# Gate and linear projections of two feed-forward blocks: seven half-width products in place of eight, on weight sums made by VectorE

## What is computed

```python
def swiglu(h, w_gu, w_dn):                       # h (512, 1024), w_gu (1024, 5632), w_dn (2816, 1024)
    g, u = jnp.split(h @ w_gu, 2, axis=-1)
    return (jax.nn.silu(g) * u) @ w_dn

x = x + 0.5 * gt1 * rmsnorm_2(swiglu(h, w_gu1[l], w_dn1[l]), g_post[l, 0])
...
x = x + 0.5 * gt3 * rmsnorm_2(swiglu(h, w_gu2[l], w_dn2[l]), g_post[l, 2])
```

## Time and profile before

| what | value |
|---|---|
| median of 3 runs | 2291.43 us (2290.36 to 2295.13) |
| the profiled execution, its own time | 2295.32 us |
| span of that execution in the profile | 2293.3 us |
| TensorE clock granted, mean | 0.987 of full |
| PE busy, share of the span | 2258.4 us, 98% |
| POOL busy | 1056.0 us, 46% |
| DVE busy | 1015.3 us, 44% |
| ACT busy | 902.7 us, 39% |

### The profile page before, as it was taken

How to read it: one execution, slowest core, us unless ns; L and a number is a source line. 1 busy time by engine, 2 the same in 40 slices (tenths; PEclk the granted TensorE clock), 3 DMA queues, 4 the chain that set the end, 5 groups by cost and what they waited for, 6 DMA issues and landing times.

```text
span 2293.3 us, 32856 instructions
## 1 busy us (share of the span) xinstructions
PE 2258.4 (98%) x10438; PEld 1858.3 (81%) x10438; DVE 1015.3 (44%) x1670; ACT 902.7 (39%) x1632; POOL 1056.0 (46%) x812
## 2 busy tenths in 40 slices
PE   8999999999999999999999999999999999999997
PEld 7888888888888888888888778888677787888886
DVE  6899785527623415110115235555565555100112
ACT  4334663333222333332333354444665453332332
POOL 3455555454444454444445443333322454444444
PEclk8999999999999999999999999999999999999999
DMA  4333444337747532333332323334312432333331
GB/s 150 97 97 96 145 120 158 96 107 288 269 134 230 174 97 78 93 100 97 96 96 83 84 80 111 110 110 142 97 51 60 149 95 74 96 96 97 96 97 60
DMA packets 129483, 263.95 MB, mean 115 GB/s; under 512 B 14256, under 2 KB 14384, under 8 KB 128624
## 3 DMA queue, kind: packets, MB, share of 16 engines
q1 hardware_dynamic: 119520, 236.51, 34.4%
q10 hardware_dynamic: 9872, 26.25, 3.0%
HBM read 250.02 MB, written 12.58 MB: 115 GB/s over the span
## 4 chain that ended last, share of the span: by engine, by line
PE 89%; DVE 5%; issue 3%; ACT 2%; POOL 1%; DMA 0%; ACTq 0%; DVEq 0%; POOLq 0%
PE bank L1028 25%; PE bank L1030 25%; PE bank L1029 25%; PE bank L1293 2%; PE bank L1294 2%; PE bank L1295 2%; PE bank L1383 1%; PE bank L1346 1%; PE bank L1427 1%; POOL wlo L415 1%; PE bank L1449 1%; DVE bank L1712 1%; PE bank L1368 1%; PE bank L1168 0%; PE bank L1131 0%
## 5 line engine op out<-in xcount | busy, mean ns | idle before, releaser
L415 POOL TENSOR_TENSOR wlo<-raw,whi 128x512 fp32r<-128x512 f32 x750 | 985.9, 1323 | 1135.2 <-ACT whi L517 1134.1
L1028 PE MATMUL bank<-a_hi,whi 128*128 128x512 f32 x1928 | 762.1, 395 | 6.5 <-DVE a_lo L1509 2.5
L1030 PE MATMUL bank<-a_lo,whi 128*128 128x512 f32 x1928 | 751.1, 390 | 0.0
L1029 PE MATMUL bank<-a_hi,wlo 128*128 128x512 f32 x1928 | 750.6, 389 | 0.0
L517 ACT ACTIVATE whi<-raw 128x512 fp32r<-128x512 f32 x750 | 468.0, 627 | 644.8 <-PE bank L1030 571.7
L1028 PEld LDWEIGHTS bank<-a_hi,whi 128*128 128x128 f32 x1928 | 362.0, 188 | 88.5 <-issue 7.2
L1030 PEld LDWEIGHTS bank<-a_lo,whi 128*128 128x128 f32 x1928 | 361.9, 188 | 76.3
L1029 PEld LDWEIGHTS bank<-a_hi,wlo 128*128 128x128 f32 x1928 | 362.2, 188 | 75.2 <-issue 1.4
L1028 PE MATMUL bank<-b_hi,whi 128*128 128x512 f32 x852 | 335.0, 393 | 0.5 <-DVE b_lo L1850 0.3
L1029 PE MATMUL bank<-b_hi,wlo 128*128 128x512 f32 x852 | 332.3, 390 | 0.0
L1030 PE MATMUL bank<-b_lo,whi 128*128 128x512 f32 x852 | 332.1, 390 | 0.0
(11 more groups left out here) (274 smaller groups left out, 1832.3 us busy)
## 6 DMA issues: line engine op xcount, KB each, us to landing
raw<-d_stream SPq DMA_DIRECT2D x750, 256.0 KB, 2.6
G<-d_ada SPq DMA_DIRECT2D x72, 512.0 KB, 5.2
spill_rv<-tmp ACTq DMA_DIRECT2D x32, 256.0 KB, 2.1
G<-spill_rv ACTq DMA_DIRECT2D x8, 1024.0 KB, 8.3
G<-d_x ACTq DMA_DIRECT2D x4, 512.0 KB, 5.6
spill_ga<-sq ACTq DMA_DIRECT2D x8, 256.0 KB, 3.7
G<-spill_ga ACTq DMA_DIRECT2D x1, 2048.0 KB, 8.4
G<-d_x ACTq DMA_DIRECT2D x1, 2048.0 KB, 13.7
```

The source lines that it names most:

```text
L415: pool.tensor_tensor(wlo[:, s % SRING, :], raw[:, s % RING, :], whi[:, s % SRING, :].bitcast(F32), ALU.subtract).then_inc(lo_done, 1)
L1028: pe.matmul(out_ps, w_hi, hi[:, k, :], start=first and q == 0, stop=False)
L1029: pe.matmul(out_ps, w_lo, hi[:, k, :], start=False, stop=False)
L1030: mm = pe.matmul(out_ps, w_hi, lo[:, k, :], start=False, stop=last and q == len(ks) - 1)
```

## The change

The gate and linear projections of the second and third feed-forward blocks, but for the first two turns (four pairs) of half a, are done by Winograd's form of Strassen's product. For two channel tiles k0, k1, the gate and the linear column tile of a pair, and the lower and upper 256 tokens, eight products of a 128 by 128 tile with 256 columns become seven: three on given weight tiles, four on sums of them. 18 of the 22 pairs of a block are done so, 36 in all.

- **PE**: `products_pair`: for each of four steps, 7 products of 3 matmuls over 256 columns, 84 for a pair, into seven halves of four banks; two sets of four banks take turns (`w_free`).
- **Stream**: for each step the load brings one panel of the four given tiles into an even `raw` slot (`given_run`, in pieces of 256 numbers); the odd slot beside it is filled by DVE with four sums (`panel_sums`, three adds in SBUF). The load waits until the odd slot is free too. ACT and POOL split both; of the given panel only three tiles (384 columns).
- **DVE and ACT at the end of a pair**: ACT copies the first product out of PSUM, DVE makes the four quarters of gate and linear part with four adds from PSUM, ACT takes silu, DVE multiplies, ACT rounds, DVE subtracts. Between these DVE makes the four panels of sums for the pair after the next one in the order of its work.
- **Token side**: sums and differences of the activation halves (`t_hi`, `t_lo`) are made by DVE and ACT once for each block, during its two turns of the old kind (`turn_values`, `turn_hi`, `turn_lo`).
- SBUF tensors get fixed addresses, `SIL` moves, one offset is rounded up to 8.

The core of the diff:

```diff
+CLASSIC = 2
+PRODUCTS = {"wg2a": 4, "wg2b": 5, "wg3a": 4, "wg3b": 5}
...
+            def given_run(name):
...
+                with sp.Fori(0, panels // 16) as i:
+                    for s in range(8):
+                        p, w, h, c = base + 2 * s, s // 4, s % 4 // 2, s % 2 * 2 * P
+                        sp.wait_ge(lo_done, i * 16 + (p + 2))
+                        at = base - sums_before(base) + 4 * h + 2 * w
+                        sp.dma_start(raw[:, p % RING, :].rearrange("p (a c) -> p a c", c=2 * P),
...
-                pool.tensor_tensor(wlo[:, s % SRING, :], raw[:, s % RING, :], whi[:, s % SRING, :].bitcast(F32),
+                c = columns_of(s)
+                pool.tensor_tensor(wlo[:, s % SRING, c], raw[:, s % RING, c], whi[:, s % SRING, c].bitcast(F32),
                                    ALU.subtract).then_inc(lo_done, 1)
...
+            def products_gates(name, skip):
...
+                def first_product(i, w):
+
+                    wait_used(act, name, i, 8 * w + 7)
+                    act.wait_ge(w_free, i * 2 + (g0 + w + 2))
+                    act.activation(WFIRST, bank[4 * (w % 2)][:, 0:H], ACT.Copy).then_inc(w_first, 1)
+
+                def silu(i, w):
+                    act.wait_ge(w_free, i * 2 + (g0 + w + 3))
+                    act.activation(WG, WG, ACT.Silu, scale=-1.0).then_inc(w_silu, 1)
...
+                def pair(i, w, before=True):
+
+                    s = 8 * w
+                    if before:
+                        first_product(i, w - 1)
+                    tick(name, i, s, 3)
+                    if before:
+                        silu(i, w - 1)
+                    tick(name, i, s + 3, 1)
+                    if before:
+                        hi(i, w - 1)
+                    tick(name, i, s + 4, 4)
...
+            def products(ps, w_slot, c, hi, lo, first, last):
...
+                pe.matmul(ps, w_hi, hi, start=first, stop=False, skip_group_check=True)
+                pe.matmul(ps, w_lo, hi, start=False, stop=False, skip_group_check=True)
+                return pe.matmul(ps, w_hi, lo, start=False, stop=last, skip_group_check=True)
...
+            def turn_values(fill, b, q):
...
+                own.next(dve.tensor_tensor(T_SRC.rearrange("p (n t) -> p n t", t=T), a_hi[:, 2 * q:2 * q + 2, :].bitcast(F32),
+                                           a_lo[:, 2 * q:2 * q + 2, :].bitcast(F32), ALU.add))
...
+            def panel_sums(name, i, s):
...
+                dve.wait_ge(raw_landed[p % RING], i * 32 + (p // RING + 1) * 16)
+                dve.wait_ge(lo_done, i * 16 + (p + 2))
+                own.next(dve.tensor_tensor(sums[:, 0:2 * P].rearrange("p (n t) -> p n t", t=P),
+                                           given[:, P:3 * P].rearrange("p (n t) -> p n t", t=P),
+                                           given[:, 0:P].rearrange("p (n t) -> p n t", t=P).to_broadcast([P, 2, P]), ALU.add))
+                own.next(dve.tensor_tensor(made[2], made[0], tile[2], ALU.add))
+                dve.tensor_tensor(made[3], made[2], tile[3], ALU.add).then_inc(raw_landed[(p + 1) % RING], 16)
+
+            def products_pair(name, i, w, skip, more):
...
+                wait_used(dve, name, i, 8 * w + 7)
+                dve.wait_ge(w_first, i * 2 + (g0 + w + 1))
+                dve.wait_ge(opb, i * 2 + (fill + skip + w))
...
+                own.next(dve.tensor_tensor(halves(u), halves(bank[at + 1][:, :]), twice(WFIRST), ALU.add))
+                own.next(dve.tensor_tensor(halves(WSUM), halves(bank[at + 3][:, :]), twice(v), ALU.add))
+                own.next(dve.tensor_tensor(g, bank[at + 2][:, :], WSUM, ALU.add))
+                dve.tensor_tensor(last, bank[at + 3][:, 0:H], WSUM[:, H:T], ALU.add).then_inc(w_free, 1)
+                if more:
+                    panel_sums(name, i, 8 * w + 16)
+                dve.wait_ge(w_silu, i * 2 + (g0 + w + 1))
+                dve.tensor_tensor(tmp[:, w % 2, :], WU, WG, ALU.mult).then_inc(w_prod, 1)
+                if more:
+                    panel_sums(name, i, 8 * w + 18)
...
+                dve.tensor_tensor(b_lo[:, b_tile, :].rearrange("p a t -> p (a t)"), tmp[:, w % 2, :],
...
+                if more:
+                    panel_sums(name, i, 8 * w + 20)
+                    panel_sums(name, i, 8 * w + 22)
```

More of the change, by code:

```diff
@@ L12 @@
+import math
 from contextlib import ExitStack
@@ L45 @@
 SOME = 4 * P
+H = T // 2
+CLASSIC = 2
+PRODUCTS = {"wg2a": 4, "wg2b": 5, "wg3a": 4, "wg3b": 5}
+PAIRS_AT = {}
+_w = 0
+for _n, _t in PRODUCTS.items():
+    PAIRS_AT[_n] = _w
+    _w += 2 * _t
 def k_panels(K, tiles):
@@ L84, with is_given, columns_of, sums_before @@
 X_FINAL = 2 * KD
+def is_given(p):
+    for name in PRODUCTS:
+        first, _, panels, _ = PLAN[name]
+        if first <= p < first + panels:
+            return (p - first) % 2 == 0
+    return False
+def columns_of(p):
+    return slice(P, SOME) if is_given(p) else slice(0, SOME)
+def sums_before(p):
+    n = 0
+    for name in PRODUCTS:
+        first, _, panels, _ = PLAN[name]
+        n += min(max(p - first, 0), panels) // 2
+    return n
+def runs_of(lo, hi):
+    cuts = [lo, hi]
+    for name in PRODUCTS:
+        first, _, panels, _ = PLAN[name]
+        cuts += [c for c in (first, first + panels) if lo < c < hi]
+    cuts = sorted(set(cuts))
+    return list(zip(cuts, cuts[1:]))
+NPANELS = NUNITS - sums_before(NUNITS)
 COLS = {}
@@ L398, in _ @@
             ada_run("gu1b", 6, 3)
-            load_run(b + 24, NPANELS - b - 24)
+            for lo, hi in runs_of(b + 24, NUNITS):
+                name = next((n for n in PRODUCTS if PLAN[n][0] == lo), None)
+                if name:
+                    given_run(name)
+                else:
+                    load_run(lo, hi - lo, -sums_before(lo))
             for k in (0, 1, 2, 6, 3, 4, 7, 5):
@@ new lines, in seven_products @@
+            def seven_products(n, norm, fill):
+                for half, K in (("a", FA), ("b", FB)):
+                    name, down = f"wg{n}{half}", f"dn{n}{half}"
+                    if half == "a":
+                        first_turn(f"gu{n}a", OPA, opa, fill, late=n == 3)
+                        for t in range(1, CLASSIC):
+                            wide_turn(f"gu{n}a", t, OPA, opa, fill)
+                    with pe.Fori(0, PRODUCTS[name]) as i:
+                        products_pair(name, i, 0, down)
+                        products_pair(name, i, 1, down)
+                    pe.wait_ge(w_free, PAIRS_AT[name] + 2 * PRODUCTS[name] + 1)
+                    for m in range(KD):
+                        tile_packed(down, m, K, OPB, opb, FILL_B[f"ffn{n}{half}"])
+                if n == 2:
+                    sums_between(0, norm)
+                else:
+                    sum_up(norm)
@@ new lines, in _, with products_gates @@
+            PAIR_STEPS = 3 + 2 * 4
+            def products_gates(name, skip):
+                turns = PRODUCTS[name]
+                for s in range(8, 16, 2):
+                    panel_sums(name, 0, s)
+                with dve.Fori(0, turns - 1) as i:
+                    own.begin(i, 2 * PAIR_STEPS)
+                    products_pair(name, i, 0, skip, True)
+                    products_pair(name, i, 1, skip, True)
+                    own.end(turns - 1)
+                products_pair(name, turns - 1, 0, skip, False)
+                products_pair(name, turns - 1, 1, skip, False)
```

221 lines of the change are left out of this document (192 added, 29 removed).

## The result

| | before | changed |
|---|---|---|
| median of 4 runs each, us | 2293.3 (2290.4 to 2295.5) | 2445.4 (2441.5 to 2448.8) |
| span of the profiled execution, us | 2293.3 | 2442.2 |
| TensorE clock granted, mean | 0.987 | 0.963 |

The ratio is 1.0663 (95% interval: 1.0641 to 1.0686): 152 us slower. Forecast were 2436 us, between 2320 and 2550, and slower with a chance of 0.90.

What follows compares the result with a forecast made beforehand. PE bounds the kernel: matmuls by their distance, 10.9 us a pair. Per block 14 x 4.5 + 4 x 1.1 plus some 5 at the start, 72; 145 for two on 2295.3, 2440, or 2436 as median; range 2320 to 2550.

Steps and rivals of the forecast that it cites:

- 84 x 0.12 = 10.1: PE's part of a pair: 84 matmuls of 256 columns, 0.12 us apart, 10.1 us (9.3 to 14.4) where it was 10.9.
- the rival with weight loads that are not hidden: PE at 256 columns: matmuls 0.171 us apart, or 0.218 with loads beside the columns, some 2560 us; chance 4%.
- 8 POOL operations hold DVE 0.85 each: In a pair, each of POOL's 8 subtractions holds up one two-SBUF-input DVE operation by 0.85 us.
- Period of 15.4: Time of a pair in the loop: DVE's 8.6 us plus 8 x 0.85 of holds, 15.4 us (11.0 to 19.4).
- PE waiting for POOL some 5 us a pair: Sign in PE's waits: some 5 us a pair for POOL's low parts (`wlo` L502), at units 6 and 7.
- The other four at 12: Four of a block's 18 pairs, first and last of each half, put at 12 us, so +1.1 each.
- Before the first pair 5 us (0 to 8): Start of each block: DVE's token sums in the second old turn make PE wait some 5 us (0 to 8).
- 72 per block: Added time per feed-forward block: 67 us from the pairs plus some 5 at the start, 145 for two.
- POOL's 384 columns 0.98: POOL's subtraction of 384 columns put at three quarters of 1.31 us, 0.98; no row showed that length.
- Transfers cost nothing: Stream loads: 256 KB land in 2.6 us, one needed each 3.8, so no cost, even if shorter pieces doubled it.
- The clock falls: Rival: PE, idle 5 us in 15, drops to half clock, 20.2 us a pair, about 2600 us; chance 8%.
- The ring's loop without the ports, 11.5: Rival: without DVE and POOL holding each other, the ring's serial loop sets 11.5 us a pair, about 2325; chance 10%.

Runs made afterwards that it cites:

- experiment 8: Changed kernel without weight sums in the loop and without token sums and differences (PE multiplies given parts instead): 2286.3 us, 0.9972 of the kernel before.
- experiment 1: Changed kernel with the loop's adds of weight sums replaced by reductions of the same columns on one SBUF input: 2335.6 us, 1.0178 of the kernel before.
- experiment 3: Changed kernel with ACT splitting units 6 and 7 ahead of silu and rounding of the pair before: 2383.9 us, 1.0389 of the kernel before.
- experiment 9: Changed kernel with ACT's splits of units 6, 7 and 8 ahead of silu, unit 9 ahead of rounding: 2365.8 us, 1.0326 of the kernel before.
- experiment 6: Changed kernel without sums and differences of activations on DVE and ACT; PE takes plain activation halves: 2421.9 us, 1.0566 of the kernel before.
- experiment 4: Changed kernel with one-input reductions for weight sums and ACT's units 6 and 7 split ahead of silu and rounding: 2320.4 us, 1.0112 of the kernel before.

## Why the prediction was right

- **"84 x 0.12 = 10.1"**: confirmed. The timeline of PE has starts 0.12 us apart, and experiment 8 runs whole pairs at 10.08:

```profile
1197.75 0.28 PE L1354 MATMUL bank<-a_hi,whi 128*128 128x256 f32 x1
1197.87 0.28 PE L1355 MATMUL bank<-a_hi,wlo 128*128 128x256 f32 x1
```

  So the rival with weight loads that are not hidden is refuted: it wanted 0.171, or 0.218 beside 256 columns. The rule of the Trainium skill behind it (TensorE: Matmul & The Clock Gate, section "The mechanism") does not describe these matmuls, each of which has its own load of 128 columns.
- **"8 POOL operations hold DVE 0.85 each"**: 8 holds, 7.1 us together in the period shown, 0.89 each. That the cause is the two SBUF inputs is shown by experiment 1, and the rule of the Trainium skill (SBUF — State Buffer, section "SBUF: two separate sides") agrees with it. Its form is seen row by row: who begins first goes on, the other waits (the last section has the counts). That there are eight because POOL is idle during the adds from PSUM is shown by experiment 3: filling this idle time left six and gave 61 us. Experiment 9 gave 18 more with as many holds, somewhat shorter ones.
- **"Period of 15.4"**: 15.4 in the stretch above, 15.1 over the 14 pairs of block two. That it came out to the tenth is luck: holds were 0.3 more than the 6.8 put down, while the 0.7 us for 18 gaps were 0.1 in the round above and 0.4 in the mean of seven rounds of half b. The mechanism is not luck: 7.8 us of work (8.6 with gaps were put down) and eight holds make the round.
- **"PE waiting for POOL some 5 us a pair"**: at units 6 and 7, as said, but less. In the six pairs above PE stands still for 4.0 us in the mean (3.2 and 4.8 in turns); 1.3 us more go by the slower clock (below).
- **"The other four at 12"**: 13.2 in the mean, and wrong by pair. By ACT's copies in block two the first pairs of the halves take 12.7 (without PE's waits at its start, below) and 10.2, the last ones 14.4 and 15.4. While the last pair runs no new sums are wanted, but DVE still makes those of this pair (its full round from 1245.07 to 1260.22); that this is the reason was not tested.
- **"Before the first pair 5 us (0 to 8)"**: too small. The timeline of block two shows four waits of PE, 9.4 us, and experiment 6, without the token side, is 12 us faster for a block:

```profile
929.36 0.80 PE L1198 MATMUL bank<-a_hi,whi 128*128 128x512 f32 x1 [2.77 <-POOL wlo L502]
...
935.79 0.38 PE L1354 MATMUL bank<-a_hi,whi 128*128 128x256 f32 x1 [1.67 <-DVE tmp L1773]
937.46 0.38 PE L1354 MATMUL bank<-t_hi,whi 128*128 128x256 f32 x1 [1.05 <-ACT G L683]
941.95 0.55 PE L1354 MATMUL bank<-t_hi,whi 128*128 128x256 f32 x1 [3.88 <-DVE tmp L1773]
```

  The step counted only DVE's time until the first pair. It left out that the later token sums (L1773) are wanted one after the other inside that pair, and that POOL is late already in the old turn (the first wait). In proportion this term was the furthest off: 9 to 12 us for 5.
- **"72 per block"**: 74.5 by the spans (148.9 for two). The terms as read in block two give 14 x (15.1 - 10.9) + 4 x (13.2 - 10.9) + 9 = 77. The period was put 0.3 too high for the 14 pairs, the other four and the start too low, and these went against one another too.
- **"POOL's 384 columns 0.98"**: 1.15 in the mean, held; 1.01 at the least.
- **"Transfers cost nothing"**: 2.7 us to land for 2.6, and none of PE's long waits is put down to one.
- **The clock falls** (a rival at 2600, with a mean under 0.9 as its sign): partly so, without its price. The mean is 0.90 in the block. Busy times around a wait; the third number from the end is the granted clock:

```profile
1201.50:1204.50 3.00, 0.00 (x0) 0.00 (x0) 2.83 (x7) 1.77 (x4) 1.36 (x1) 1.00 0.00 0
1204.50:1207.50 3.00, 2.76 (x14) 2.47 (x15) 2.86 (x4) 1.88 (x4) 2.50 (x3) 0.66 0.00 0
1207.50:1210.50 3.00, 3.00 (x22) 3.00 (x21) 2.86 (x4) 1.16 (x3) 2.90 (x3) 0.77 0.38 98
```

  After some 4 us of idle PE the mean is 0.66, then 0.77: part of the time at 1.2 GHz, the rest at 2.4. PE's matmuls start 0.21 us apart for some 3.5 us of this pair and 0.12 otherwise; over the six pairs above that is 1.3 us a pair. The rival assumed that the clock stays down for the whole pair. That the 1.3 us cost nothing is argued from DVE's row, which is full all the same; no run tested it by itself.
- **"The ring's loop without the ports, 11.5"**: not the first bound. Experiments 1 and 4, where the sums don't meet POOL, stand at 11.2 and 11.0. That is near the 11.5 of this loop, but the order of 4 was to cut the loop and hardly changed the period, so that the loop is the next bound is not shown.

The parts, from the bottom up: the products alone 2286 (-6), with the token side 2303 (+17), with DVE's time for the sums and the longer ring loop 2336 (+32), with the hold between DVE and POOL 2445 (+110). The 32 us between the second and the third were not taken apart. In the orders of experiments 3 and 9 DVE's row is as full as in the changed kernel (94% of its rounds), so it is most likely still the bound. What stays open is what sets the 11.0 to 11.2 us of experiments 1 and 4, where DVE is idle for 2 to 4 us of each round.

## What to carry to other kernels

Before work is moved from a full engine to two idle ones, look whether they can work at the same time: here DVE and POOL, with 7.8 and 9.2 us of work for a pair, came to 15.4, as each POOL operation held up one DVE operation on two SBUF inputs. Weigh such a change by its ceiling first, the gain with the added work for nothing: seven products for eight at half the width gave 6 us of 2292, as 84 matmuls of 0.12 are hardly less than 48 of 0.227. Where a hold can't be avoided, put the held engine's PSUM work beside the other engine's busy stretch; moving two and then four splits of ACT ahead gave back 61 and then 79 of the 152 us. And take a busy share over whole rounds of the loop: in experiment 9 DVE is busy 94% of its rounds, but 81% of 1140 to 1250 us, since the last pair of half b ends at 1227.

## What the runs showed beyond that

- A reduction on one SBUF input runs unheld beside POOL: 0.414 and 0.287 us, with POOL's operation of 512 columns at 1.319.
- Who begins first decides. Of the 432 adds of weight sums in the changed kernel (L1849, L1852, L1853), 243 began while an operation of POOL ran, and each of them was held: 1.22 us in the mean, 0.48 the one that began just as POOL ended. The other 189 began ahead of POOL's operation or with POOL idle, and took 0.41 to 0.43 us at 256 columns and 0.29 to 0.30 at 128.
- So the same operation is held in one run and not in another, as its start falls: the product with two SBUF inputs (0.69 us) was never held in the changed kernel and takes 1.59 in experiment 4; the subtraction of the low part is at 1.49 in the changed kernel and 0.693 in experiment 1.
- A hold for which nobody waits is nearly free: the 12 adds for a pair in the kernel before cost 0.35 us for a pair.
